# Prompt attention of a sparse-attention decoder step: two key copies moved, query tiles in another order

## The reference, cut to what matters

```python
def _masked_softmax(s, mask):
    s = jnp.where(mask, s.astype(jnp.float32), NEG)
    m = jnp.max(s, axis=-1, keepdims=True)
    e = jnp.where(mask, jnp.exp(s - m), 0.0)
    return e / jnp.maximum(jnp.sum(e, axis=-1, keepdims=True), 1e-30)
...
    p = _masked_softmax(s, (cend[None, :] <= qpos[:, None])[None, :, None, None, :])
    o_c = jnp.einsum('btgrn,bngd->btgrd', p.astype(q.dtype), comp[:, :, 1])
...
    o_s = jnp.einsum('bgtrnj,bgtnjd->btgrd', p.astype(q.dtype), kvg[..., 1, :])
...
    o_w = jnp.einsum('btgrl,blgd->btgrd', p.astype(q.dtype), kvw[:, :, 1])
    o = g[..., 0:1] * o_c + g[..., 1:2] * o_s + g[..., 2:3] * o_w
```

## Time and profile before

| | us |
|---|---|
| median of 3 runs (805.85 to 807.83) | 807.26 |
| the profiled execution | 806.2 |
| its span, first to last instruction | 804.5 |
| PE busy | 735.1 (91%) |
| DVE busy | 417.6 (52%) |
| ACT busy | 295.5 (37%) |
| POOL busy | 110.5 (14%) |

### The profile page before, as it was taken

How to read it: one execution, slowest core, us unless ns; L and a number is a source line. 1 busy time by engine, 2 the same in 40 slices (tenths; PEclk the granted TensorE clock), 3 DMA queues, 4 the chain that set the end, 5 groups by cost and what they waited for, 6 DMA issues and landing times.

```text
span 804.5 us, 15333 instructions
## 1 busy us (share of the span) xinstructions
PE 735.1 (91%) x6221; PEld 534.0 (66%) x6221; DVE 417.6 (52%) x920; ACT 295.5 (37%) x794; POOL 110.5 (14%) x178
## 2 busy tenths in 40 slices
PE   0889999999998999999978899999999999998995
PEld 0857699999985778855545565666766677664441
DVE  0746568888873143203374576666444444443544
ACT  0327344444441011100155556563333333562411
POOL 2300160000000000000088202112112121000000
PEclk9999999999999999999999899999999999979998
DMA  9995934444000311220066710002176767332121
GB/s 247 335 347 213 403 139 157 157 158 157 1 1 1 97 40 53 79 86 1 1 219 284 293 58 1 2 1 93 56 239 230 243 219 248 130 137 64 53 88 44
DMA packets 37529, 108.09 MB, mean 134 GB/s; under 512 B 5715, under 2 KB 21122, under 8 KB 36307
## 3 DMA queue, kind: packets, MB, share of 16 engines
q1 hardware_dynamic: 31699, 56.77, 21.2%
q0 software_dynamic: 5760, 50.33, 16.8%
HBM read 101.80 MB, written 11.55 MB: 141 GB/s over the span
## 4 chain that ended last, share of the span: by engine, by line
PE 77%; DMA 5%; DVE 5%; POOL 4%; SPq 3%; ACT 3%; issue 2%; POOLq 0%; ACTq 0%; DVEq 0%
PE ps L902 13%; PE ps L1086 8%; PE ps L1084 8%; PE ps L1400 7%; PE ps L1230 6%; DMA wcols<-in_w_ada 5%; PE ps L879 5%; PE ps L1161 3%; PE ps L1311 3%; PE ps L1112 3%; PE ps L1136 2%; PE ps L1295 2%; PE ps L1243 2%; SPq L675 2%; PE ps L1256 2%
## 5 line engine op out<-in xcount | busy, mean ns | idle before, releaser
L902 PE MATMUL ps<-xd,w 128*128 128x192 f32 (+1 forms) x512 | 93.0, 325 | 0.0
L902 PEld LDWEIGHTS ps<-xd,w 128*128 128x128 f32 x512 | 84.8, 190 | 0.0
L879 PE MATMUL ps<-ident,cache 128*128 128x128 f32 x384 | 54.3, 279 | 20.0 <-DMA w<-in_phi_w 19.1
L1086 PE MATMUL ps<-wcols,hT 128*128 128x384 f32 (+1 forms) x192 | 66.8, 507 | 3.0 <-issue 3.0
L1230 PE MATMUL ps<-zw,hT 128*128 128x256 f32 x256 | 65.2, 396 | 3.1 <-ACT z_gate L1640 2.2
L1084 PE MATMUL ps<-hT,wcols 128*128 128x288 f32 x256 | 64.7, 410 | 0.0
L879 PEld LDWEIGHTS ps<-ident,cache 128*128 128x128 f32 x384 | 46.2, 145 | 25.8 <-issue 23.3
L1415 ACT COPY xt<-ps 64x384 f32<-64x384 f32 x64 | 30.2, 471 | 85.2 <-PE ps L879 84.9
L1950 DVE TENSOR_REDUCE peak<-ps 128x2 f32<-128x1024 f32 (+3 forms) x48 | 39.5, 823 | 36.5 <-PE ps L1115 36.5
L1603 ACT ACTIVATE probs<-ps,peak 128x512 f32<-128x512 f32 (+3 forms) x96 | 49.9, 526 | 19.6 <-DVE peak L1950 19.2
L1086 PEld LDWEIGHTS ps<-wcols,hT 128*128 128x128 f32 x192 | 36.8, 194 | 30.3 <-issue 15.1
(11 more groups left out here) (332 smaller groups left out, 1183.9 us busy)
## 6 DMA issues: line engine op xcount, KB each, us to landing
wcols<-in_w_ada SPq DMA_DIRECT2D x6, 2048.0 KB, 10.5
win_rows<-in_state_win_kv SPq DMA_DIRECT2D x8, 768.0 KB
out<-in_state_win_kv SPq DMA_DIRECT2D x1, 6048.0 KB
zw<-in_w_in SPq DMA_DIRECT2D x4, 1024.0 KB, 6.6
wcols<-in_w_in SPq DMA_DIRECT2D x2, 1536.0 KB, 12.4
w_o<-in_w_out SPq DMA_DIRECT2D x1, 3072.0 KB, 11.3
w<-in_phi_w SPq DMA_DIRECT2D x4, 512.0 KB, 8.7
x_rows<-in_x_prompt SPq DMA_DIRECT2D x1, 2048.0 KB, 16.5
```

Of the source, the lines that this page charges most:

```text
L879: last = pe.transpose(ps[:, (2 * n + j) % 3, c * P:(c + 1) * P], caches[b % 2][:, 2 * s + j, c * P:(c + 1) * P], ident[:])
L902: last = pe.matmul(out, w[:, k, :], x[:, k * G:(k + 1) * G, 0:width], start=(s == 0 and k == 0), stop=(s == JP - 1), skip_group_check=True)
L1086: last = pe.matmul(ps[:, job_bank[j], 0:width], hT[:, c, t * P:(t + 1) * P], w[:, c, col:col + width], **flags)
```

## The change

The table `KT` now also names the semaphore that each copy counts in (0 for those that ACT copies, 1 for DVE's), and set 4 counts for ACT. ACT copies set 4 after the exponentials of unit 1; DVE copies set 5 alone, at n = 2, behind the maximum of unit 2 and the copy of unit 0's transposed probabilities. PE waits for sets 4 and 5 no longer ahead of the scores of unit 3 but ahead of its first value matmul, in the same turn. A table `T_ORDER` gives the tiles in the order 3, 0, 2, 1 for the first pair of heads and 1, 2, 0, 3 for the second, in the list of units and in POOL's loop.

```diff
--- before.py
+++ after.py
@@ -355,15 +355,16 @@
             k += 1
         assert z_solid[DB - 1] == [NZ - 1]
 
-        KT = [(0, 2), (G, 3), (2, 4), (4, 5), (1, 6), (5, 7)]
+        KT = [(0, 2, 0), (G, 3, 1), (2, 4, 0), (4, 5, 0), (1, 6, 0), (5, 7, 1)]
         assert G == 3 and len(KT) == 2 * G
         MH = H // 2
+        T_ORDER = ((3, 0, 2, 1), (1, 2, 0, 3))
+        assert NT == 4 and R == 4
         units = []
         for g in range(G):
             units.append(("cmp", g, None, None, None))
             for m in range(g * R // 2, (g + 1) * R // 2):
-                for k in range(NT):
-                    t = k if m % (R // 2) else NT - 1 - k
+                for t in T_ORDER[m % (R // 2)]:
                     for s in range(2):
                         units.append(("full", g, m, t, s))
         NU = len(units)
@@ -645,7 +646,7 @@
 
             for j in range(MH * NT):
                 m, k = divmod(j, NT)
-                t = k if m % (R // 2) else NT - 1 - k
+                t = T_ORDER[m % (R // 2)][k]
                 rows = nsa[:, t, m * P:(m + 1) * P]
                 if j % (R // 2 * NT) == 0:
                     pool.wait_ge(cmp_added, 2 * (m * 2 // R) + 2)
@@ -1177,7 +1178,7 @@
             pe.wait_ge(pcomp_made, 1)
             score(0)
             pe.wait_ge(job_out[1], count[1])
-            for x, bank in KT:
+            for x, bank, _ in KT:
                 s, g = divmod(x, G)
                 if bank == 5:
                     pe.wait_ge(u_last_out, 1)
@@ -1193,14 +1194,15 @@
                         pe.wait_ge(kt_made[e], 1)
                 if 1 <= n <= 3:
                     pe.wait_ge(kt_made[0], n)
-                if n == 3:
-                    pe.wait_ge(kt_made[1], 3)
                 if 1 <= n < NU:
                     score(n)
                 if 2 <= n < NU + 2:
                     turn_probs(n - 2)
                 if n >= 4 and units[n - 4][4] == 1:
                     turn_heads(n - 4)
+                if n == 3:
+                    pe.wait_ge(kt_made[0], 4)
+                    pe.wait_ge(kt_made[1], 2)
                 if 3 <= n < NU + 3:
                     value(n - 3)
 
@@ -1462,14 +1464,14 @@
                 last.then_inc(job_out[e], 1)
 
         def copy_keys(eng, copy, k):
-            x, bank = KT[k]
+            x, bank, e = KT[k]
             s, g = divmod(x, G)
             eng.wait_ge(u_last_turned, 1)
             eng.wait_ge(cmp_stored, 16)
             eng.wait_ge(stored, 16)
             eng.wait_ge(kt_turned, k + 1)
             copy(kT[0:d, s, g, :], ps[0:d, bank, :])
-            copy(kT[d:P, s, g, :], ps[0:d, bank, :]).then_inc(kt_made[x % 2], 1)
+            copy(kT[d:P, s, g, :], ps[0:d, bank, :]).then_inc(kt_made[e], 1)
 
         def copy_prompt_pairs(eng, s):
             for j in range(2):
@@ -1604,8 +1606,8 @@
                                                   ACT.Exp, bias=peak[n % 2][:, h:h + 1],
                                                   accum_out=total[:, m, t, s, h:h + 1])
                     last.then_inc(probs_made, 1)
-                if n == 0:
-                    copy_keys(act, act.copy, 3)
+                if n < 2:
+                    copy_keys(act, act.copy, 3 + n)
                 if 3 <= n < NU + 3:
                     kind, g, m, t, s = units[n - 3]
                     done = full_upto[n - 3] + 2 * cmp_upto[n - 3]
@@ -1978,8 +1980,7 @@
                                                     cshare[:].rearrange("p (t h) -> p t h", h=R), gate, ALU.mult))
                     dve.tensor_tensor(rows, rows, cshare[:].unsqueeze(2).to_broadcast([P, NT * R, PC]), ALU.mult)\
                        .then_inc(cmp_made, 1)
-                if n == 1:
-                    copy_keys(dve, dve.tensor_copy, 4)
+                if n == 2:
                     copy_keys(dve, dve.tensor_copy, 5)
                 if n >= 4 and n - 4 < NU and units[n - 4][4] == 1:
                     j = full_upto[n - 4] // 2 - 1
```

## The result

| | before | after |
|---|---|---|
| median of 22 runs each, in turns | 805.92 (803.71 to 808.63) | 809.12 (807.97 to 814.47) |
| ratio after/before, 95% interval | | 1.0046 [1.0031, 1.0061] |
| profiled execution, its span | 806.2, 804.5 | 808.44, 806.7 |

The changed kernel is 0.46% slower. The time lies inside the range, and the forecast of 808.1 is 1.0 off; but I forecast +0.9 us against before, and measured are +3.2, which is outside of what I called no change. That 808.1 comes so near is luck: it was built on the median of three runs, 807.26, and the 22 runs put before at 805.92, 1.3 lower. So the size has to be found, and it isn't all where I looked.

The account below looks back on a forecast made before the run. TensorE work bounds nearly throughout, with POOL's release at 443.5 holding the first group. Terms 0 + 0.9 + 0.4 - 2.1 + 2.4 - 1.1 + 0.4 = +0.9 us; forecast 808.1 against 807.26, range 804.9 to 810.6.

Parts of the forecast that it names:

- Key copies: the term is 0: Start of the first head group: 2.09 us of TensorE idle goes, but waiting for POOL grows; 0, bounds -2.1 and 0.
- POOL's date: First head group: POOL releases VectorE's buffer at 443.5, set by no attention engine; TensorE idles 5.27 us behind it.
- Query tiles, +0.9: Prompt attention: the new tile order leaves TensorE's work unchanged and alters waits in five places; with the copies' 0, +0.9 us.
- Term 1: Two boundaries between head groups: a tile-0 value matmul covers 0.44 less of the wait; +0.44 at each, +0.9.
- term 2: Tail of prompt attention: a shorter value matmul no longer covers VectorE's copy, so TensorE waits; +0.4.
- terms 3 and 4: TensorE's waits for copied heads in three groups: old ones go, -2.1; new ones ahead of tile 3 come, +2.4 (0 to +3).
- Term 5: First group behind POOL's release: less TensorE work left, -1.1; wider first VectorE maximum and copy, +0.4.
- Both causes stay, so I book no change: TensorE at 1.2 GHz behind POOL's release and the stage's end: no change; one 3.4-us stretch is worth 1.7.
- the third rival: Both group boundaries: longer waits take the clock down to 1.2 GHz, 1.7 us each; 811.5, chance 0.13.
- The start's gain arrives: First group: if POOL doesn't hold it, 2.1 us and the half-clock stretch go; 802.6, chance 0.05.
- No new waits for the heads: Prompt attention: ScalarE copies the heads in time in the new places, so +2.4 becomes 0; 805.7, chance 0.13.
- One stretch more or less elsewhere: Behind POOL's release or at the stage's end: one half-clock stretch more or less; 806.4 or 809.8, chance 0.07.

Follow-up runs that it names:

- order alone: Kernel before with only the new query tile order, keys copied as before: 806.12, ratio 1.0005 [0.9976, 1.0034] against before.
- the two of before: Profiles of the kernel before and of it with one needless TensorE wait added in turn 2, instruction count unchanged; the latter measured 807.96, ratio 1.0013.
- copies alone: Changed kernel with the old tile order: 809.33, ratio 1.0031 against before; again with a needless TensorE wait removed, instruction count unchanged: 811.98, 1.005.
- the three of the whole change: Profiles of the changed kernel, its repeat on another chip (811.18, ratio 1.0053), and it without a needless TensorE wait (810.27, 1.0053).
- the gathers moved: POOL's eight gathers put behind its first eight pairs of adds: on before 798.89; with new copies 800.4; with new order 801.81; with both 803.32.
- after once more: The unaltered changed kernel measured again on the chip of the follow-up kernels, against before: 811.18, ratio 1.0053 [1.0032, 1.0074].

## Why the prediction was right or wrong

*"Key copies: the term is 0", with POOL's date.* Right for the prompt's stage, and the reason is shown: the date is 39.11 to 39.15 behind POOL's start in all nine profiles that have it, score 3 comes earlier, the wait at the release grows, and P is the same within 0.3 in the mean. Without the date the gain appears in P at 2.5 to 2.9, more than the 2.09 of the idle time; part of it is clock, 3.4 and 6.8 us at 1.2 GHz in P against 10.2. The bounds of this term, -2.1 and 0, were drawn too narrow at the other end: they had no room for a cost outside the stage, and E took 4.0 more in the mean. This is the step that failed most: I followed the edit to the end of the stage that it is in, and not what its instructions, one of them on TensorE, change behind it.

*Query tiles, +0.9.* Term 1 measured +0.44 at a boundary (1.25 against 0.81; the group as a whole 45.29 and 45.30 against 44.86), term 2 +0.46, and terms 3 and 4 together +0.4 against +0.3: right. Mis-sized was their sum in P, +0.9 to +2.1 (order alone against the two of before, after against the two with copies alone). What the sum left out is the next point. Term 5, the work ahead of POOL's date, shows no clear gain: from the release to the next group took 14.81 with the order alone against 15.20 and 15.64 in the two of before, but 15.58 to 16.13 in the three of the whole change against 15.75 and 16.07 with the copies alone. (Its +0.4 is also smaller than its own row gives: 384 columns at 1.35 ns are 0.5.) Without the date the order has one more cost, which I didn't see: with a tile 0 as the third score TensorE waits another 0.73 and 0.48 right behind it, in the two kernels with the gathers moved and the new order and in none of the three others.

*"Both causes stay, so I book no change" for the clock.* Wrong. The trace of before has a third stretch at 0.50 in this stage that I didn't read, 3.4 us from 416.8 on; its like lasts 0 to 10.2 in the fourteen profiles, with old copies and new. Behind the release the 0.50 lasted 10.2 us in after instead of 6.8, and so it did in five of the six profiles with the new copies and the date (6.8 in the sixth), against 6.8, 3.4 and 10.2 in the three with the old. Inside a group it was new, one of the things that I had named as a sign of being wrong:

```profile
507.40:510.80 3.40, 3.40 (x18) 2.50 (x18) 1.14 (x4) 0.59 (x1) 0.00 (x0) 0.50 0.00 0
```

That is the third rival, at one boundary instead of both: five of the six profiles with the order 3,0,2,1 and 1,2,0,3 have such a stretch, 1.8 to 2.4 us behind the first cmp score of the second or third group, and none of the eight others. It starts ahead of the 1.25-us wait that I had blamed; what TensorE did before is the new wait for the heads just ahead of the cmp scores, 0.87 at 459.57 and 0.59 at 504.86, then two microseconds of narrow scores. It cost 0.4 to 1.0 (the second group is 45.99 with it, in after once more, and 45.29 without, the stretch behind it 52.79 and, with the gathers moved, 52.24 against 51.83), not 1.7; part of it is paid out of the boundary's wait of 1.25, which is 0 to 0.69 where the stretch runs over it. The Trainium skill, "TensorE: Matmul & The Clock Gate", section "A second HAM failure mode: psum-queue depth-cycling", tells of short frequent idle times that make the clock swing without one long gap. The five stretches fit that, but the same waits stand at twelve boundaries of the six profiles, and only five of them show a stretch.

*The other rivals.* The start's gain arrives: no, as long as POOL has its date. No new waits for the heads: no, of 3.0 us in all, 0.87, 0.59 and 0.59 are at the three places of term 4. One stretch more or less elsewhere: yes, in both senses; the one behind the release is longer, and the one at the end of the stage is gone from S (0 in all three profiles of the whole change).

Summed by profiles (means of three of the whole change and two of before): P +1.9, S -1.8, E +3.1, together +3.2 (and +0.8 at the start, ahead of the first edited line); the medians of the runs say +3.2 on one chip and +4.5 on another (ratios 1.0046 and 1.0053). Shown is where the time is: the tile order in P and the end of the sequences' stage, E. That the pattern of waits in E goes with the key copies is shown by fourteen profiles without an exception, and its length by their means, with an overlap; *through what* they do it, the list's length or another of their effects, stays open, as does why one wait of 2 us in E leaves the clock down longer in most profiles than the stop of 0.90 to 1.23 does.

## What to carry to other kernels

Look for the engine that sets a date: a helper engine's queue with work ahead of what others wait for (eight gathers whose rows are first read near 557 us) was worth 7.6 us, while two edits of the pipeline that waited for it were worth less than nothing. A gain ahead of such a date is a longer wait. And compare the whole span after an edit, stage by stage with the granted clock, not only the stage that was edited: here most of the cost lay 150 us behind it.

## What the runs showed of the hardware

- While the program runs, 50 packets of a queue of kind "instruction" move by DMA (0.82 MB, in each of the fourteen profiles). Where one of them started 0.40 to 0.64 us ahead of the mask matmul, beside the load of `w_o`, TensorE stopped for 0.90 to 1.23 us, shown as idle time by "issue" (five profiles); where it started 2.80 to 4.13 us ahead, TensorE didn't (nine). That TensorE waited for this packet is read from the times and not shown.
- Whether an added wait lengthens an engine's list couldn't be read from the source here: one wait more in turn 2 left 15333 instructions; two more on the first value matmul and one less on a score made it 15334.
- The same 12.9 us of VectorE's and 14.9 us of ScalarE's work at the end of the sequences' stage took 22.09 us at a mean clock of 0.92 and 28.21 at 0.70: 13.7 us more at 1.2 GHz, worth up to 6.9, against a difference of 6.1.
